# A one-core decoder step, last stage: closing norm by tokens, last two slabs by output tiles, middle norm's squares added by VectorE, first output tiles side by side

## What is computed

```python
def _rmsnorm(x, g):
    y = x * lax.rsqrt(jnp.mean(x * x, axis=-1, keepdims=True) + EPS)
    return y * g

mixed = (g_a * y_a + g_b * y_b) @ w_out
x = x + gate1 * mixed
h = _rmsnorm(x, g_ffn) * (1.0 + scale2) + shift2
a, b = jnp.split(h @ w_gu, 2, axis=-1)
x = x + gate2 * ((silu(a) * b) @ w_down)
y = _rmsnorm(x, g_final)
```

## Time and profile before

| | us |
|---|---|
| median of 3 runs | 1169.84 (1168.84 to 1169.90) |
| the profiled execution | 1163.87 |
| its span in the trace | 1162.1 |
| PE busy | 1060.5 (91% of the span) |
| DVE, ACT busy | 526.0, 539.1 (45%, 46%) |

### The profile page before, as it was taken

How to read it: one execution, slowest core, us unless ns; L and a number is a source line. 1 busy time by engine, 2 the same in 40 slices (tenths; PEclk the granted TensorE clock), 3 DMA queues, 4 the chain that set the end, 5 groups by cost and what they waited for, 6 DMA issues and landing times. The chain is left out here.

```text
span 1162.1 us, 25596 instructions
## 1 busy us (share of the span) xinstructions
PE 1060.5 (91%) x9313; PEld 915.2 (79%) x9313; DVE 526.0 (45%) x1160; ACT 539.1 (46%) x1058; POOL 82.5 (7%) x59
## 2 busy tenths in 40 slices
PE   7789986758999999999999999988998999999996
PEld 3578865547777877777777778778997899999994
DVE  1500015523636454554546363657654754445315
ACT  3313224744565756566656574553432544443212
POOL 1143410001010000000000000000000000000000
PEclk9789995877999999999999999988999899999998
DMA  9797767318566666656574746764652344444301
GB/s 331 210 307 252 244 229 262 131 65 314 165 234 214 213 224 208 227 195 239 175 259 162 278 137 227 218 187 130 222 184 88 96 156 155 153 159 148 111 0 46
DMA packets 129908, 219.49 MB, mean 189 GB/s; under 512 B 19348, under 2 KB 74129, under 8 KB 125058
## 3 DMA queue, kind: packets, MB, share of 16 engines
q1 hardware_dynamic: 124962, 185.14, 48.2%
q0 software_dynamic: 4896, 33.68, 8.0%
HBM read 210.46 MB, written 12.45 MB: 192 GB/s over the span
## 5 line engine op out<-in xcount | busy, mean ns | idle before, releaser
L103 PE MATMUL ps<-b_uH,b_slabH 128*128 128x320 f32 x480 | 151.9, 316 | 11.8 <-DVE b_uL L547 7.5
L1207 PE MATMUL ps<-t_XT,t_slab 128*128 128x128 f32 x1024 | 145.3, 282 | 11.2 <-DVE t_XT L1654 10.1
L104 PE MATMUL ps<-b_uL,b_slabH 128*128 128x320 f32 x480 | 150.4, 313 | 0.0
L105 PE MATMUL ps<-b_uH,b_slabL 128*128 128x320 f32 x480 | 149.7, 312 | 0.0
L1207 PEld LDWEIGHTS ps<-t_XT,t_slab 128*128 128x128 f32 x1024 | 129.4, 195 | 22.4 <-issue 10.5
L2079 ACT ACTIVATE b_slabH<-t_slab 128x2048 fp32r<-128x2048 f32 (+1 forms) x52 | 92.3, 1783 | 99.7 <-PE ps L105 92.6
L2182 DVE TENSOR_TENSOR b_slabL<-t_slab,b_slabH 128x2048 fp32r<-128x2048 f32 (+1 forms) x52 | 109.1, 2123 | 62.3 <-ACT b_slabH L2079 62.3
L103 PEld LDWEIGHTS ps<-b_uH,b_slabH 128*128 128x128 f32 x480 | 91.9, 191 | 14.5 <-issue 11.6
L1503 ACT ACTIVATE t_KTr<-ps 128x512 f32<-128x512 f32 x152 | 82.1, 592 | 22.7 <-PE ps L1231 19.7
L104 PEld LDWEIGHTS ps<-b_uL,b_slabH 128*128 128x128 f32 x480 | 92.2, 192 | 0.0
L105 PEld LDWEIGHTS ps<-b_uH,b_slabL 128*128 128x128 f32 x480 | 92.0, 192 | 0.0
(11 more groups left out here) (381 smaller groups left out, 2081.8 us busy)
## 6 DMA issues: line engine op xcount, KB each, us to landing
t_Kr<-cache_moba_kv SPq DMA_DIRECT2D x132, 256.0 KB, 3.0
t_Vr<-cache_moba_kv SPq DMA_DIRECT2D x124, 256.0 KB, 5.7
t_slab<-w_ada SPq DMA_DIRECT2D x22, 1024.0 KB, 7.4
t_slab<-w_gu SPq DMA_DIRECT2D x22, 1024.0 KB, 5.3
t_slab<-w_in SPq DMA_DIRECT2D x17, 1024.0 KB, 6.4
t_slab<-w_down SPq DMA_DIRECT2D x11, 1024.0 KB, 5.1
t_slab<-cmp_w SPq DMA_DIRECT2D x2, 2048.0 KB
t_wkv<-cache_nsa_win SPq DMA_DIRECT2D x8, 512.0 KB, 3.2
```

The costliest lines, as they stand in the source:

```text
L103: pe.matmul(out, w_high, x_high, start=start, stop=False, **kw)
L104: pe.matmul(out, w_high, x_low, start=False, stop=False, **kw)
L105: return pe.matmul(out, w_low, x_high, start=False, stop=stop, **kw)
L1207: return pe.matmul(out[:, P * j:P * j + P], taps(w, j, lp)[:, P * ht:P * ht + P], XT[:, w, lp, j, :, :].rearrange("p v i -> p (v i)"), sta ...
```

## The change

1. First gates: the two output tiles are made side by side, three matmuls for one and three for the other, channel tile after channel tile (`first_gates`).
2. Output projection: behind each `residual` DVE also makes x * amp in `uT` (two instructions), and from m = 2 adds the square of tile m - 1 to the first square (`add_square`). Two matmuls with ones are left of the middle `square_norm`: one on the sum, one on the last tile's square.
3. After the reciprocal DVE multiplies by root, adds the shift and subtracts; x * amp is already there.
4. The first group of up products is written out ahead of the loop and makes its four output tiles side by side, channel tile after channel tile (`first_up`).
5. Down products: the last two slabs are worked output tile by output tile, 12 matmuls each, in the order 4, 5, 6, 7, 0, 1, 2, 3, so that a bank closes every 12 matmuls; both slabs must be split before the first.
6. Closing: ACT makes x * g in `uT` itself, behind each square; PE turns this not yet normalized y, 12 transposes ahead of the last two output tiles, 9 behind them, 3 at the end. DVE adds up the squares except for the last tile's. Six matmuls with one moving column (`token_sum`) give the sum for each token on its partition, so root and reciprocal are taken of 128 x 1 columns, and the copies out of PSUM multiply by it. All copies have banks of their own.

```diff
+            def first_gates():
+                for kk in range(KT):
+                    if kk % 2 == 0:
+                        pe.wait_ge(u_split, kk // 2 + 1)
+                        if kk == 4:
+                            split(0)
+                    for m in range(2):
+                        last = split_matmul(pe, ps[4 * m][:, 0:TOK], *weights(0, 256 * kk + P * m), uH[:, kk, :],
+                                            uL[:, kk, :], kk == 0, kk == KT - 1)
+                        if kk == KT - 1:
+                            last.then_inc(gate_mm, 1)
+            first_gates()
...
-            square_norm(pe, t["ones"], sq, ps[7], sq_done, 0, ss_mm)
+            for n, part in enumerate((0, KT - 1)):
+                if n:
+                    pe.wait_ge(sq_done, KT)
+                else:
+                    pe.wait_ge(sq_added, KT - 2)
+                last = pe.matmul(ps[7][:, 0:TOK], t["ones"][:, :], sq[:, part, :], start=n == 0, stop=n == 1)
+            last.then_inc(ss_mm, 1)
...
-                            if group == f == half == 0:
-                                pe.wait_ge(h_split, k + 1)
...
+            def first_up():
+                split(N_GU)
+                split(N_GU + 1)
+                for kk in range(KT):
+                    pe.wait_ge(h_split, kk + 1)
+                    for f in range(2):
+                        for half in range(2):
+                            last = split_matmul(pe, ps[2 * f + half][:, 0:TOK], *weights(N_GU + half, 256 * kk + P * f),
+                                                uH[:, kk, :], uL[:, kk, :], kk == 0, kk == KT - 1)
+                            if kk == KT - 1:
+                                last.then_inc(b_mm if half else a_mm, 1)
+            first_up()
+            up(0, 1)
+            with pe.Fori(1, 5) as it:
...
-            down(N_DOWN + 9, 0, 18)
-            down(N_DOWN + 10, 0, 20, final=True)
-            pe.wait_ge(x_done, KT + 4)
-            square_norm(pe, t["ones"], sq, ps[7], sq_done, KT, ss_mm, (4, 5, 6, 7, 0, 1, 2, 3))
-            for j in range(6):
-                i, half = j // 2, j % 2
-                pe.wait_ge(y_done, 4 * half + 4)
+            split(N_DOWN + 9)
+            split(N_DOWN + 10)
+            ORDER = (4, 5, 6, 7, 0, 1, 2, 3)
+            def turned(tiles, half):
+                for m in tiles:
+                    pe.wait_ge(y_done, ORDER.index(m) + 1)
+                    for i, (t0, n) in enumerate(T_TILES):
+                        last = pe.transpose(ps[5 + i if half else i][0:n, P * (m % 4):P * (m % 4) + P], uT[:, m, t0:t0 + n], ident[:, :])
+                return last
+            def token_sum(i, part, start):
                 t0, n = T_TILES[i]
-                if j >= 2:
-                    pe.wait_ge(y_dve if half else y_act, i)
-                for k in range(4):
-                    last = pe.transpose(ps[half][0:n, P * k:P * k + P], uT[:, 4 * half + k, t0:t0 + n], ident[:, :])
-                last.then_inc(y_tr, 1)
+                return pe.matmul(ps[3 + i % 2][0:n, i:i + 1], sq[:, part, t0:t0 + n], t["ones"][:, 0:1], start=start, stop=not start)
+            for j, m in enumerate(ORDER):
+                for n in (9, 10):
+                    for f in range(2):
+                        last = split_matmul(pe, ps[m][:, 0:TOK], *weights(N_DOWN + n, D * f + P * m), GH[:, 2 * n + f, :],
+                                            GL[:, 2 * n + f, :], False, n == 10 and f == 1, skip_group_check=True)
+                last.then_inc(last_mm, 1)
+                if j == 5:
+                    pe.wait_ge(x_done, KT + 4)
+                    turned(ORDER[0:4], 1).then_inc(y_tr, 1)
+            pe.wait_ge(x_done, KT + 7)
+            turned(ORDER[4:7], 0)
+            pe.wait_ge(sq_added, KT - 2 + KT - 2)
+            token_sum(1, 4, True)
+            pe.wait_ge(x_done, 2 * KT)
+            token_sum(0, 4, True)
+            pe.wait_ge(sq_done, 2 * KT)
+            token_sum(0, 3, False)
+            token_sum(1, 3, False)
+            token_sum(2, 4, True)
+            token_sum(2, 3, False).then_inc(ss_mm, 1)
+            turned(ORDER[7:8], 0).then_inc(y_tr, 1)
...
+                act.activation(uT[:, k, :], xT[:, k, :], ACT.Copy, scale=t["vecT"][:, V_GZ + k:V_GZ + k + 1]).then_inc(y_done, 1)
+            act.wait_ge(ss_mm, 2)
             for i, (t0, n) in enumerate(T_TILES):
-                act.wait_ge(y_tr, 2 * i + 1)
-                act.activation(yn[0:n, i, 0:512], ps[0][0:n, :], ACT.Copy).then_inc(y_act, 1)
+                act.activation(t["root"][0:n, i:i + 1], ps[3 + i % 2][0:n, i:i + 1], ACT.Sqrt, bias=t["eps"][0:n, 0:1],
+                               scale=1.0 / D).then_inc(root_done, 1)
+            act.wait_ge(y_tr, 2)
+            act.wait_ge(r_done, 1)
+            for i, (t0, n) in enumerate(T_TILES):
+                act.activation(yn[0:n, i, 0:512], ps[i][0:n, :], ACT.Copy, scale=t["root"][0:n, i:i + 1]).then_inc(y_act, 1)
...
+            def add_square(m):
+                dve.wait_ge(sq_done, m + 1)
+                dve.wait_ge(sq_added, m - 1)
+                dve.tensor_tensor(sq[:, 0, :], sq[:, 0, :], sq[:, m, :], ALU.add).then_inc(sq_added, 1)
+            amp = t["amp"]
             dve.wait_ge(x_back, 16)
             for m in range(KT):
                 dve.wait_ge(mix_mm, m + 1)
                 residual(m, ps[m % 2], 16, 0, m)
+                dve.wait_ge(x_done, m + 1)
+                dve.tensor_scalar(uT[:, m, 0:SEQ], xT[:, m, 0:SEQ], amp[:, 1, m, 0:1], None, ALU.mult)
+                dve.tensor_tensor(uT[:, m, SEQ:TOK].rearrange("p (b t) -> p b t", t=T),
+                                  xT[:, m, SEQ:TOK].rearrange("p (b t) -> p b t", t=T),
+                                  amp[:, 1, m, 1:9].unsqueeze(2).to_broadcast([P, NB, T]), ALU.mult).then_inc(h_mid, 1)
+                if 2 <= m:
+                    add_square(m - 1)
...
-            modulate(dve, t, 1, 24, h_pre, h_mid, h_done, h_high, h_split)
+            dve.wait_ge(h_mid, KT)
+            for step in range(KT + 2):
+                if step < KT:
+                    dve.tensor_tensor(uT[:, step, :], uT[:, step, :], t["root"][:, :], ALU.mult).then_inc(h_pre, 1)
+                m = step
+                if m < KT:
+                    dve.wait_ge(h_pre, m + 1)
+                    dve.tensor_scalar(uT[:, m, 0:SEQ], uT[:, m, 0:SEQ], mod[:, 24 + m, 0:1], None, ALU.add)
+                    h = uT[:, m, SEQ:TOK].rearrange("p (b t) -> p b t", t=T)
+                    dve.tensor_tensor(h, h, mod[:, 24 + m, 1:9].unsqueeze(2).to_broadcast([P, NB, T]), ALU.add)\
+                       .then_inc(h_done, 1)
+                m = step - 1
+                if 0 <= m < KT:
+                    dve.wait_ge(h_high, m + 1)
+                    dve.tensor_tensor(uL[:, m, :], uT[:, m, :], uH[:, m, :], ALU.subtract).then_inc(h_split, 1)
...
+                if i >= 2:
+                    dve.wait_ge(sq_done, KT + i)
+                    dve.wait_ge(sq_added, KT - 2 + i - 2)
+                    dve.tensor_tensor(sq[:, 4, :], sq[:, 4, :], sq[:, (3 + i) % 8, :], ALU.add).then_inc(sq_added, 1)
+            dve.wait_ge(root_done, 4)
+            dve.reciprocal(t["root"][0:64, 2:3], t["root"][0:64, 2:3])
+            dve.reciprocal(t["root"][:, 0:2], t["root"][:, 0:2]).then_inc(r_done, 1)
+            dve.wait_ge(r_done, 1)
+            dve.wait_ge(y_tr, 1)
             for i, (t0, n) in enumerate(T_TILES):
-                dve.wait_ge(y_tr, 2 * i + 2)
-                dve.tensor_copy(yn[0:n, i, 512:1024], ps[1][0:n, :]).then_inc(y_dve, 1)
+                dve.tensor_scalar(yn[0:n, i, 512:1024], ps[5 + i][0:n, :], t["root"][0:n, i:i + 1], None, ALU.mult).then_inc(y_dve, 1)
```

More of the change, by code:

```diff
@@ L1842, in _ @@
             dve.wait_ge(emptied_dve, PRO_DVE + (NB - 1) * N_DVE + len(by_dve(LAST)))
-def square_norm(pe, ones, sq, bank, sq_done, first, ss_mm, order=range(KT)):
-    for i, k in enumerate(order):
-        pe.wait_ge(sq_done, first + i + 1)
-        last = pe.matmul(bank[:, 0:TOK], ones[:, :], sq[:, k, :], start=i == 0, stop=i == KT - 1)
-    last.then_inc(ss_mm, 1)
 def back_block(nc, sem, t, d, ps):
@@ L1868, in back_block @@
     a_mm, b_mm, silu_done, f_step, f_done = sem("b_a_mm"), sem("b_b_mm"), sem("b_silu"), sem("b_f_step"), sem("b_f")
-    last_mm = sem("b_last_mm")
+    last_mm, r_done = sem("b_last_mm"), sem("b_r")
     down_mm, y_done, y_tr, y_act, y_dve, dve_step, stored = (sem("b_down_mm"), sem("b_y"), sem("b_y_tr"), sem("b_y_act"),
@@ L1952, in mix @@
             def mix(i, it):
-                if not isinstance(it, int) or i:
-                    split(i, it)
+                split(i, it)
                 for m in range(2):
@@ L1967, in mix @@
                     for k in range(KT if i < 2 else 4):
-                        if isinstance(it, int) and i == m == 0 and k % 2 == 0:
-                            pe.wait_ge(u_split, k // 2 + 1)
-                            if k == 4:
```

(21 more changed lines are left out.)

3 lines of the change are left out of this document (1 added, 2 removed).

## The result

The change makes the kernel faster: 1152.53 us as the median of four runs (1150.76 to 1158.28) against 1169.87 for the kernel before (four runs, 1168.84 to 1170.87), a ratio of 0.9866 [0.9839, 0.9892] (in brackets, here and below, the 95% interval). The gain is under 2% and clear of the scatter. Measured twice more, the same kernel gave ratios of 0.9901 [0.9881, 0.9921] and 0.9856 [0.9831, 0.9882]. Over all measurements of this study the medians are 1168.84 for before (43 runs) and 1153.96 for after (16 runs): 14.9 us, a little less than the 17.3 of the first measurement.

The account below looks back on a forecast made before the run. PE, busy 91% of the span, bounds the kernel, with the stretch behind its last product. Middle 1.85 us won (1.0 + 1.3 + 3.7 - 4.15) plus closing 9.6 makes 11.45, so 1169.84 becomes 1158.4, range 1154.8 to 1161.0.

Parts of the forecast that it names:

- First gates, 0.: First gates: PE did not wait for channel tiles, so taking two output tiles side by side frees nothing, 0.
- Output projection, the pause.: Output projection: DVE waits for ACT's late square, so PE starts tile 5 2.25 us late, tile 6 adds 0.45; 2.7 together.
- I take the fall.: Output projection: the clock falls in the pause before tile 5, 1.9 us for 16 slower matmuls; 2.25 + 1.9 = 4.15 lost.
- The old pauses: Trace of before: clock 0.50 behind pauses of 1.87 and 2.24 us, 1.00 behind 3.59 us; two of three fell.
- rival 1: Output projection: the pause comes but the clock stays; 1.45 us less, 1156.9; chance 0.27.
- Middle norm and first tile of h.: Between output projection and up products: norm 1.0 us won by fewer matmuls with ones, first tile of h 1.3 won.
- First group of up products.: First 96 up matmuls, side by side: PE no longer waits, 16 at 0.267 and 80 at 0.147 us, 3.7 won.
- Closing.: Last slabs, norm and stores: early transposes 1.4 us, copies done T + 5.6, stores serial, end T + 10.5; 9.6 won.
- Sum.: Whole last stage: 1.85 us won in the middle plus 9.6 in the closing, 11.45 us.
- I subtract from the median.: Whole kernel: nothing in the change touches the 6.0 us between profiled execution and median, so 1169.84 - 11.45 = 1158.4.
- The 1.1 us between the three runs shown: Range: runs before lie 1.1 us apart, so within 0.2% (2.3 us) no difference can be told.

Follow-up runs that it names:

- Both ways of removing its cause: Changed kernel with additions of squares 1 to 4 later on DVE, 1151.09 us; changed kernel with ACT's first two squares ahead of the second `high_gu`, 1152.35 us.
- early squares: Changed kernel with ACT's table load and squares of tiles 0 and 1 ahead of the second `high_gu`: 1152.35 us, ratio 0.9852.

## Why the prediction was wrong, by its steps

- **First gates, 0.** Right: 100.07 us in the old order, 100.11 in the new.
- **Output projection, the pause.** Right in place and mechanism, and 2.75 us where 2.7 was forecast (tile 5 2.19 late for 2.25, tile 6 another 0.48 for 0.45). Both ways of removing its cause removed it.
- **"I take the fall."** This is the step that failed, the largest error in the sum. The term was 4.15 lost; measured 2.75, as the clock stayed at 1.00. The old pauses spoke for a fall, and more than the prediction says: behind the pause of 3.59 us it read 1.00 from a stretch that ends at 235.50, but the same trace has 0.89 in 235.50 to 236.00 and 0.50 in 236.00 to 240.00, so that pause is no case without a fall and does not speak for rival 1. None of the three stood in work like this: behind the first PE was busy for 1.47 of 3.00 us, behind the third for some 2 us and then for 1.00 of 4.00 (236.00 to 240.00), and in the 50 us around the second (240 to 290 us) for 37.67, at a clock of 0.77 on average. That this is what makes the difference is not shown. The nearest pause was not weighed at all. It stands in the trace of before, in the same output projection, with PE full behind it:

```profile
865.97 0.42 PE L103 MATMUL ps<-b_zH,b_slabH 128*128 128x320 f32 x1 [1.64 <-DVE b_zL L2239]
...
865.97:867.47 1.50, 1.50 (x10) 1.50 (x11) 1.50 (x1) 0.00 (x0) 0.00 (x0) 1.00 0.04 11
```

  The clock stayed at 1.00 from there to 880 us, with PE busy all the time. In eight traces with the pause of 2.03 us the clock fell behind it once. Rival 1, on this row and not on the one it named, should have been the forecast: 1.4 us.
- **Middle norm and first tile of h.** 2.3 won forecast, 2.47 measured.
- **First group of up products.** 3.7 forecast, 4.37 measured. PE does not wait, as said; ten or eleven matmuls ran at the lower clock in place of the assumed 16. That number moved between executions (15.4 to 16.8 us for the group), so the term was good only to about 1 us.
- **Closing.** 9.6 forecast, 10.3 measured. Early transposes 1.31 against 1.4. Copies done at T + 5.67 against T + 5.6. The data of the first store moved 0.85 us behind its issue and not 1.17, the three stores took 3.73 and not 3.84, the end 0.9 and not 1.0: T + 9.9 in place of T + 10.5.
- **Sum.** 11.45 + 1.40 (fall) + 0.17 (norm and h) + 0.67 (group) + 0.69 (closing) - 0.17 (gates) = 14.21, what the traces give. Nearly all errors had one sign.
- **"I subtract from the median."** This rests on the stretch ahead of the last stage being the same in both. It scatters. The first gate matmul stood between 759.18 and 766.61 us in fourteen traces, before at 760.51, in a program that is the same up to there. The profiled execution of before, 1163.87 us, is as fast as the fastest of its 43 runs (1163.88 to 1173.02); that of after, 1153.42, is near its median. The 1.1 us between the three runs shown was no measure of that scatter, so the range was too narrow. The first measurement's 17.3 us is the 14.2 of the traces and some 3 of scatter; with the right 14.2 the forecast would have been 1155.6, and 1168.84 - 14.2 = 1154.6 from the pooled median of before, against 1153.96 measured. So two things put 1152.53 below the range: terms that were 2.8 us too small together, half of it the fall, and this scatter of 3 us, which no term had. Either alone would have left the time inside.

What sets the 7 us of scatter was not tried and stays open. The traces show what goes with it. In the stretch 170 to 300 us, in the attention part, the granted clock was 0.76 in the two traces that reached the first gate matmul soonest (759.18 and 760.51, the second being that of before), 0.72 in ten (762.33 to 766.11) and 0.71 in two (765.81 and 766.61). So much of the scatter goes with how long the clock is low there; which of the two brings about the other is not shown, and 3.8 us of scatter within the ten stay unexplained.

## What to carry to other kernels

When one engine takes over a sum from another, the wait goes to the place of the addition, and everything behind it on that engine waits too: look at what the engine that delivers has queued ahead of its first item, and put the additions behind that. A closing norm that is linear in its last factor can be moved behind the transposes, to token sums of one column and a scale in the copies; working the last slabs by output tile, so that banks close no faster than the next engine empties them, was worth about as much. And compare traces from a common instruction on: here ahead of the touched stage lay 7 us of scatter, half as much as the whole gain.

## What the runs showed of the hardware

**The same pause does not always bring the clock down.** The pause of 1.62 us in the first output tile is in all fourteen traces, with the same work ahead of it; behind it the granted clock fell in two (0.67 and 0.72 in the next 2 us, then 0.50) and stayed at 1.00 in twelve. Behind that of 2.03 us it fell in one of eight. One execution fell behind the shorter pause and, 18 us later, not behind the longer. Each fall cost 1.1 to 1.5 us. The Trainium skill (TensorE: Matmul & The Clock Gate, "Why this matters for your kernels") says that only idle gaps longer than these bring the lower level back; nineteen of the twenty-two passages agree with it and three do not. So it was the better guide here than the rows that I weighed against it, two of which (pauses of 1.87 and 2.24 us, each with 0.50 behind it) do contradict it, and it is not a sure one.

**How long the clock is low in the gates varies too.** In two of fourteen traces (one store left out, early squares) the stretch from the first gate matmul to the output projection took 103.7 to 103.8 us in place of 100. In that of the early squares the clock fell in 781 to 784 (0.60 on average) and was at 0.50 until about 798; with one store left out it was at 0.50 from 778.8 to 795.8; in after it fell at 786 and rose at about 796. So it was low for about 17 us there and for 10 in after. One of the two had reached the first gate matmul soonest of all (759.18), but before, at 760.51, took 99.94, so an early start alone does not bring this about; the cause is open. This is one more reason to repeat executions rather than to read one.

**One moving column costs nearly as much as 128.** Twelve instructions of token sums with one moving column took 1.38 us at the upper clock, 0.115 each, and nine instructions of transposes with 128 columns 1.14, 0.127 each.
